# Compressing keys and values with two tokens in the contraction and two head groups side by side

## The chip, the cores and the metric

The kernel is one program on 1 core of a Trainium2 chip. The metric is the device time of one execution in microseconds (us). Times of a run are compared with those of the kernel before.

## The reference

One inference step of a two-layer decoder, for a prompt of 512 tokens and 8 sample sequences of 4 new tokens each, whose past of 256 tokens lies in pages of a cache. Layer 0 mixes tokens by retention and a spatial gate; layer 1 is sparse attention. One of its branches first compresses keys and values, and this is what the change touches:

```python
CMP_LEN, CMP_STRIDE = 32, 16        # NSA_KV = 4 groups, HEAD_DIM = 64
def compress(rows, pe_k, pe_v, phi_k, phi_v):      # rows: [k, v] of each token
    ...
    kb = blocks[:, :, :, 0] + pe_k[:, None, :]
    vb = blocks[:, :, :, 1] + pe_v[:, None, :]
    kc = jnp.einsum('bnlgd,lde->bnge', kb, phi_k)
    vc = jnp.einsum('bnlgd,lde->bnge', vb, phi_v)
    return kc, vc
```

A block is 32 consecutive tokens, and a new one begins every 16 tokens: 31 blocks in the prompt, 15 in each sample sequence (from its pages). For every group, each block is contracted over its 32 tokens `l` and 64 dims `d` with a kernel `phi[l, d, e]`. Everything is float32.

## The kernel before

Five engines run instruction streams that are written by hand, with semaphores between them. The order on each engine is the order of the code. Activations lie transposed (dims on partitions, tokens in columns), and the large products split each float32 into a high and a low part: ScalarE writes the high part of a weight unit (`split_hi`, tile `wH`), VectorE the low part (`split_lo`, `wL`), TensorE makes three products in fp32r. SyncE loads the weight units (`load_unit`) into `raw`, which has two slots: unit u is loaded once `wL` of unit u-2 is written. A product lands in one of two PSUM slots, `gemm`, which must be evacuated before it is used again.

The compression runs in two places.

**The sample sequences, in layer 0's output projection** (`project_out(E_OUT, 1, 1)`: 4 weight units, 8 chunks). Layer 1's cached pages are brought in here, beside layer 0's work. GpSimd loads 16 pages one by one (`load_page`): it reads a page number from the table, then issues a DMA of 256 KB. There are 4 page buffers. Before each chunk but the first, and after the last one, TensorE transposes two pages (`turn_pages`), 4 squares of 128x128 each; ScalarE copies them to `cT` (`take_pages`). SyncE loads the kernels `phiK`, `phiV` ahead of the last weight unit, after VectorE has cleared them: the two groups of a pair stand on a block diagonal of a 128x128 weight, so half of each weight is zeros. `compress(z, l0, l1)` then does one float32 matmul of 255 columns for each token place l (8 sequences, 2 pairs of groups, 15 blocks, and 15 columns for the position bias). Parts of `compress` stand among the steps of the norm that follows: behind the square sums of the projection, between the 8 square sums of the next norm (`square_sum(2, m, sqm)`), and around `spread_rstd(2)`, which sends the norm's factor to all partitions. VectorE then fills the input of the first feed-forward unit (`norm_fill`), piece by piece, and TensorE's `feature_chunk` waits for each piece.

**The prompt, in layer 1's input projection** (11 weight units from `O_IN`, each of 5 chunks for 5 tiles of tokens, but for one of gates). GpSimd clears `phiK2`, `phiV2` and loads them, behind two small tables and ahead of a copy of `win_sample` (4 MB from DRAM to DRAM). All six loads count on one semaphore, `o_in`. VectorE waits for it before its first rotary step, since that needs the tables `cosO` and `sinO`; `split_lo` of the next weight unit stands behind. After unit 3, TensorE transposes the prompt's rows (`turn_rows`), ScalarE copies them to `cPT`; after units 5 and 7 `compress_prompt(z)` does 32 float32 matmuls of 62 columns.

A float32 matmul shows as two records in the trace (two weight loads, two passes).

## Time and profile before

| | |
|---|---|
| median of 3 runs | 1756.84 us (1748.97 to 1760.66) |
| the profiled execution | 1754.42 us |
| its span, first to last instruction | 1752.6 us |
| mean granted TensorE clock | 0.959 of full speed |
| TensorE busy | 1622.1 us, 93% |
| VectorE, ScalarE, GpSimd busy | 781.5, 687.5, 228.5 us |
| moved by DMA | 140.56 MB, mean 80 GB/s |

The profiled execution takes 1.8 us more than its span, and lies 2.4 us under the median. In all views PE is TensorE's matmul stream and PEld its weight loads, DVE is VectorE, ACT ScalarE, POOL GpSimd, SP SyncE; a q behind it is the engine's sequencer. L801 is line 801 of the kernel before. Transposes are L556, VectorE's and ScalarE's helpers stand under one line each (L1499 the low parts, L1157 all of ScalarE's).

### The profile page before, as it was taken

What the parts mean: (1) busy time and instruction counts of PE and PEld (TensorE: products, weight loads), DVE (VectorE), ACT (ScalarE), POOL (GpSimd) and SP (SyncE); (2) the same over time, 40 slices, a digit from 0 to 9 for tenths busy, and PEclk for the clock granted to TensorE, in tenths of its full rate; (3) what the DMA queues carried; (4) which work ended last, traced back from release to release, by engine and by line L of the source; (5) the groups of instructions that cost most, each with busy time, mean ns of one, the idle gap of its engine ahead of it and who ended that gap; (6) DMA issues with size and microseconds to landing.
All of it is one profiled execution on the core that took longest, in us unless ns stands there. A gap on an engine that the chain in (4) does not pass through costs nothing.

```text
span 1752.6 us, 31047 instructions
## 1 busy us (share of the span) xinstructions
PE 1622.1 (93%) x12951; PEld 1483.6 (85%) x12951; DVE 781.5 (45%) x1251; ACT 687.5 (39%) x1303; POOL 228.5 (13%) x586
## 2 busy tenths in 40 slices
PE   4999988999999999978899889898869999999996
PEld 2989977799999999977899756565859999999995
DVE  2565453355542455343212366653236553255523
ACT  4123123345542455223222365655235553255422
POOL 3000001200000000002010344432100000000000
PEclk8999999999999999987999899999879999999998
DMA  6122318213323322324432210004211323332231
GB/s 207 49 74 96 97 55 170 83 29 92 87 78 107 82 76 78 90 86 86 174 112 59 51 50 1 1 1 145 59 48 49 96 73 95 89 96 74 72 88 51
DMA packets 189975, 140.56 MB, mean 80 GB/s; under 512 B 15505, under 2 KB 181665, under 8 KB 189809
## 3 DMA queue, kind: packets, MB, share of 16 engines
q1 hardware_dynamic: 179632, 107.36, 22.0%
q0 software_dynamic: 10240, 31.80, 6.4%
q8 instruction: 69, 1.13, 0.3%
q14 instruction: 34, 0.27, 0.0%
HBM read 130.32 MB, written 13.01 MB: 82 GB/s over the span
## 4 chain that ended last, share of the span: by engine, by line
PE 79%; DVE 8%; ACT 4%; DMA 4%; issue 3%; POOL 2%; POOLq 1%; SPq 0%; DVEq 0%; ACTq 0%
PE gemm L847 39%; PE gemm L581 17%; PE gemm L597 8%; PE misc L556 4%; PE gemm L982 1%; PE misc L1013 1%; DMA raw<-in_o_w_in 1%; ACT pr L1157 1%; POOLq L489 1%; DVE pr L1800 1%; DVE hL L1510 1%; DVE y L1527 1%; DVE y L1517 1%; PE misc L935 1%; PE misc L617 1%
## 5 line engine op out<-in xcount | busy, mean ns | idle before, releaser
L1499 DVE TENSOR_TENSOR wL<-raw,wH 128x2048 fp32r<-128x2048 f32 (+2 forms) x107 | 222.1, 2076 | 260.1 <-ACT wH L1157 260.1
L847 PE MATMUL gemm<-hH,wH 128*128 128x272 f32 x1280 | 268.4, 291 | 0.0
L847 PE MATMUL gemm<-hH,wL 128*128 128x272 f32 x1280 | 264.8, 288 | 0.0
L847 PE MATMUL gemm<-hL,wH 128*128 128x272 f32 x1280 | 264.0, 288 | 0.0
L1157 ACT ACTIVATE wH<-raw 128x2048 fp32r<-128x2048 f32 (+2 forms) x107 | 185.3, 1732 | 70.1 <-PE gemm L581 31.1
L847 PEld LDWEIGHTS gemm<-hH,wH 128*128 128x128 f32 x1280 | 200.6, 188 | 6.0 <-issue 5.0
L847 PEld LDWEIGHTS gemm<-hL,wH 128*128 128x128 f32 x1280 | 201.1, 188 | 0.0
L847 PEld LDWEIGHTS gemm<-hH,wL 128*128 128x128 f32 x1280 | 199.9, 189 | 0.0
L597 PE MATMUL gemm<-wH,hH 128*128 128x256 f32 x560 | 165.3, 295 | 15.6 <-DVE hL L1510 8.5
L1720 DVE SCALAR_TENSOR_TENSOR conv<-up,rows_t,conv 128x560 f32<-128x560 f32 x88 | 70.6, 802 | 218.4 <-ACT conv L1157 218.4
L597 PE MATMUL gemm<-wL,hH 128*128 128x256 f32 x560 | 162.9, 291 | 0.0
L597 PE MATMUL gemm<-wH,hL 128*128 128x256 f32 x560 | 161.7, 289 | 0.0
L581 PE MATMUL gemm<-hH,wH 128*128 128x272 f32 (+1 forms) x656 | 142.0, 298 | 7.5 <-DVE hL L1510 3.9
L581 PE MATMUL gemm<-hH,wL 128*128 128x272 f32 (+1 forms) x656 | 137.8, 292 | 0.0
L581 PE MATMUL gemm<-hL,wH 128*128 128x272 f32 (+1 forms) x656 | 137.7, 292 | 0.0
L1157 ACT ACTIVATE up<-gemm 128x32 f32<-128x32 f32 (+2 forms) x264 | 66.0, 324 | 175.9 <-PE gemm L847 154.4
L597 PEld LDWEIGHTS gemm<-wH,hH 128*128 128x128 f32 x560 | 109.9, 196 | 20.6 <-DVE hL L1510 7.2
L581 PEld LDWEIGHTS gemm<-hH,wH 128*128 128x128 f32 (+1 forms) x656 | 105.0, 192 | 13.6 <-issue 8.6
L597 PEld LDWEIGHTS gemm<-wH,hL 128*128 128x128 f32 x560 | 110.9, 198 | 0.0
L597 PEld LDWEIGHTS gemm<-wL,hH 128*128 128x128 f32 x560 | 110.2, 197 | 0.0
L847 PE MATMUL gemm<-aH,wH 128*128 128x272 f32 x528 | 110.2, 290 | 0.0
L847 PE MATMUL gemm<-aL,wH 128*128 128x272 f32 x528 | 108.9, 287 | 0.0
(332 smaller groups left out, 2720.5 us busy)
## 6 DMA issues: line engine op xcount, KB each, us to landing
raw<-in_f_w_in SPq DMA_DIRECT2D x88, 512.0 KB, 5.0
raw<-in_f_w_out SPq DMA_DIRECT2D x32, 704.0 KB, 4.6
raw<-in_e_w_in SPq DMA_DIRECT2D x12, 1024.0 KB, 5.1
raw<-in_o_w_in SPq DMA_DIRECT2D x10, 1024.0 KB, 5.2
raw<-in_e_w_out SPq DMA_DIRECT2D x4, 1024.0 KB, 6.2
pages<-in_cache_cmp POOLq DMA_DIRECT2D x16, 256.0 KB, 5.1
raw<-in_o_w_out SPq DMA_DIRECT2D x16, 256.0 KB, 5.7
rows<-in_cache_sel POOLq DMA_DIRECT2D x12, 256.0 KB, 3.0
```

The lines of the kernel that those rows point to most:

```text
L489: page = eng.value_load(a["page_table"][b:b + 1, pg:pg + 1], min_val=0, max_val=N_POOL - 1)
L556: ins = pe.transpose(out, in_, ident[base:base + k, base:base + k])
L581: ins = pe.matmul(gemm[c % 2][0:m, n, 0:TH], w, x[:, k, n * TH:(n + 1) * TH], start=(n_k == 0 and part == 0), stop=(n_k == nk - 1 and part ...
L597: ins = pe.matmul(gemm[c % 2][:, 0, 0:width], x, w, start=(k == 0 and part == 0), stop=(k == DC - 1 and part == 2))
L617: ins = pe.matmul(misc[:, 1 + q // 2, (q % 2) * TQ:(q % 2 + 1) * TQ], spread[:, q, :], rr[:, :], start=True, stop=True)
L847: ins = pe.matmul(gemm[odd][:, n, 0:TH], w, x[:, k, n * TH:(n + 1) * TH], start=(k == 0 and part == 0), stop=(k == nk - 1 and part == 2))
L935: ins = pe.matmul(b7[:, z * 2 * NCP:(z + 1) * 2 * NCP], (phiK2, phiV2)[z][:, l, :], cPT[:, 2 * z:2 * z + 2, l:l + 16 * (NCP - 1) + 1:16], ...
L982: ins = pe.matmul(slot[:, g2, 0:keys], qTs[j][half, r, rows], (ksT, kwT)[br][half, j, 0:keys], start=True, stop=True)
L1013: ins = pe.matmul(misc[64 * g2:64 * g2 + 64, 2 + grp % 2, r * P:(r + 1) * P], kvN[:, 1 + kt, (2 * br + 3) * 256 + g * HD:(2 * br + 3) * 25 ...
L1157: order(act.activation(out, in_, func, **kw), sem_)
L1499: order(dve.tensor_tensor(unit_view(wL, u), unit_view(raw, u), unit_view(wH, u).bitcast(F32), ALU.subtract), lo_ready)
L1720: order(dve.scalar_tensor_tensor(conv[:, j, :], U[:, j, 1:1 + CW], w[:, 17:18], conv[:, j, :], ALU.mult, ALU.add))
```

## The change

- `phiK`, `phiV`, `phiK2`, `phiV2` become [128 x 16 x 64]: the partitions hold two consecutive tokens' 64 dims. Nothing is zero, so nothing is cleared, and each is loaded by two DMAs of 256 KB in place of two of 512 KB. SyncE's loads wait for the barrier before the projection, no longer for VectorE.
- `compress` and `compress_prompt` go over 16 token pairs. For each pair two matmuls with 64 output columns follow each other, one for each group of the pair (`g2`), into partitions 0 to 63 and 64 to 127.
- A page is loaded to 64 partitions, two tokens on each, 4 KB per partition. VectorE copies the two pages of a sequence to `pairs`, so that one partition holds two tokens side by side; there are two slots. These 16 copies stand after `split_lo` of each of the 4 units. TensorE waits for `paired`, GpSimd reuses a page buffer after `paired`.
- Position tables: two DMAs in place of four.
- `turn_rows` uses four PSUM banks and waits for no copy; ScalarE makes 16 copies of 64x256 in place of 4 of 128x512.

```diff
-        phiK, phiV = sb("phiK", [P, CL, P]), sb("phiV", [P, CL, P])
-        cT = sb("cT", [P, 2, 16, 2 * DB + 1, 16])
-        pages = sb("pages", [P, 4, 512], at=top - 2 * FH * P * 4)
+        phiK, phiV = sb("phiK", [P, CL // 2, HD]), sb("phiV", [P, CL // 2, HD])
+        cT = sb("cT", [P, 2, 8, 2, 2 * DB + 1, 16])
+        pairs = sb("pairs", [P, 2, 2, G, 2 * HD])
+        pages = sb("pages", [P, 2, 2, 2, G, HD], at=top - 2 * FH * P * 4)
...
                 if u == E_OUT + 3:
-                    sp.wait_ge(phi_clear, 2)
+                    sp.wait_ge(phase, 2 * N_BAR)
                     for z, phi in enumerate((phiK, phiV)):
-                        name = ("o_phi_k", "o_phi_v")[z]
-                        for g in range(2):
-                            sp.dma_start(phi[64 * g:64 * g + 64, :, 64 * g:64 * g + 64], a[name][0].rearrange("l d e -> d l e")).then_inc(phi_in, 16)
+                        src = a[("o_phi_k", "o_phi_v")[z]][0].rearrange("(t l) d e -> l d t e", l=2)
+                        for l in range(2):
+                            sp.dma_start(phi[64 * l:64 * l + 64, :, :], src[l]).then_inc(phi_in, 16)
...
+                pe.wait_ge(paired, first // 2 + 1)
                 for n in (first, first + 1):
-                    pe.wait_ge(page_in[n % 4], 16 * (n // 4 + 1))
                     if n >= 2:
                         pe.wait_ge(page_ev, n - 1)
-                    for zj in range(4):
-                        turn(misc[:, 1 + n % 2, zj * P:(zj + 1) * P], pages[:, n % 4, zj * P:(zj + 1) * P], page_turned if zj == 3 else None)
+                    for g in range(G):
+                        turn(misc[:, 1 + n % 2, g * P:(g + 1) * P], pairs[:, (n // 2) % 2, n % 2, g, :], page_turned if g == 3 else None)
...
                 for l in range(l0, l1):
-                    ins = pe.matmul(out, (phiK, phiV)[z][:, l, :], cT[:, z, l % 16, :, l // 16:l // 16 + NCS],
-                                    start=(l == 0), stop=(l == CL - 1))
+                    for g2 in range(2):
+                        ins = pe.matmul(out[64 * g2:64 * g2 + 64, :], (phiK, phiV)[z][:, l, :], cT[:, z, l % 8, g2, :, l // 8:l // 8 + NCS],
+                                        start=(l == 0), stop=(l == CL // 2 - 1))
...
-            compress(0, 4, 8)
+            compress(0, 2, 4)
             for m in range(DC):
                 square_sum(2, m, sqm)
-                compress(0, 8 + 3 * m, 11 + 3 * m)
-            compress(1, 0, 8)
+                compress(0, 4 + 3 * m // 2, 4 + 3 * (m + 1) // 2)
+            compress(1, 0, 4)
             spread_rstd(2)
-            compress(1, 8, CL)
+            compress(1, 4, CL // 2)
...
                 for z in range(4):
-                    if z >= 2:
-                        pe.wait_ge(cp_ev, z - 1)
                     for t in range(4):
-                        turn(misc[:, z % 2, t * P:(t + 1) * P], kvN[:, t + 1, z * P:(z + 1) * P], cp_turned if t == 3 else None)
+                        turn(misc[:, z, t * P:(t + 1) * P], kvN[:, t + 1, z * P:(z + 1) * P], cp_turned if t == 3 else None)
...
-                for l in range(CL):
-                    ins = pe.matmul(b7[:, z * 2 * NCP:(z + 1) * 2 * NCP], (phiK2, phiV2)[z][:, l, :],
-                                    cPT[:, 2 * z:2 * z + 2, l:l + 16 * (NCP - 1) + 1:16], start=(l == 0), stop=(l == CL - 1))
+                for l in range(CL // 2):
+                    for g2 in range(2):
+                        ins = pe.matmul(b7[64 * g2:64 * g2 + 64, z * 2 * NCP:(z + 1) * 2 * NCP], (phiK2, phiV2)[z][:, l, :],
+                                        cPT[:, z, l % 8, g2, :, l // 8:l // 8 + NCP], start=(l == 0), stop=(l == CL // 2 - 1))
...
                     for z in range(4):
                         act.wait_ge(cp_turned, z + 1)
-                        activate(cPT[:, z, :], misc[:, z % 2, :], ACT.Copy, cp_ev)
+                        for g2 in range(2):
+                            tokens = misc[64 * g2:64 * g2 + 64, z, :].rearrange("p (u s l) -> p l s u", s=8, l=2)
+                            for l in range(2):
+                                activate(cPT[64 * l:64 * l + 64, z // 2, :, g2, z % 2, :], tokens[:, l, :, :], ACT.Copy, cp_ev if g2 and l else None)
...
                         dve.wait_ge(phase, 2 * N_BAR)
-                        for phi in (phiK, phiV):
-                            order(dve.memset(phi[:, :, :], 0.0), phi_clear)
-                        order(dve.memset(cT[:, :, :, 2 * DB, :], 0.0), pe_clear)
+                        for z in range(2):
+                            order(dve.memset(cT[:, z, :, :, 2 * DB, :], 0.0), pe_clear)
+                    if first == E_OUT:
+                        for b in (2 * i, 2 * i + 1):
+                            for n in (2 * b, 2 * b + 1):
+                                dve.wait_ge(page_in[n % 4], 16 * (n // 4 + 1))
+                            if b >= 2:
+                                dve.wait_ge(page_turned, 2 * (b - 1))
+                            for l in range(2):
+                                order(dve.tensor_copy(pairs[:, b % 2, :, :, HD * l:HD * l + HD], pages[:, b % 2, l]), paired if l else None)
...
                 if n >= 4:
-                    pool.wait_ge(page_turned, n - 3)
+                    pool.wait_ge(paired, n // 2 - 1)
                 page = pool.value_load(a["page_table"][n // NPG:n // NPG + 1, n % NPG:n % NPG + 1], min_val=0, max_val=N_POOL - 1)
-                pool.dma_start(pages[:, n % 4, :], a["cache_cmp"][0, page].rearrange("t z g d -> t (z g d)")).then_inc(page_in[n % 4], 16)
+                pool.dma_start(pages[64 * (n % 2):64 * (n % 2) + 64, (n // 2) % 2],
+                               a["cache_cmp"][0, page].rearrange("(t l) z g d -> t l z g d", l=2)).then_inc(page_in[n % 4], 16)
...
-            for phi in (phiK2, phiV2):
-                order(pool.memset(phi[:, :, :], 0.0))
-            order.wait()
             for phi, name in ((phiK2, "o_phi_k"), (phiV2, "o_phi_v")):
-                for g in range(2):
-                    pool.dma_start(phi[64 * g:64 * g + 64, :, 64 * g:64 * g + 64], a[name][0].rearrange("l d e -> d l e")).then_inc(o_in, 16)
+                src = a[name][0].rearrange("(t l) d e -> l d t e", l=2)
+                for l in range(2):
+                    pool.dma_start(phi[64 * l:64 * l + 64, :, :], src[l]).then_inc(o_in, 16)
```

VectorE at layer 0's output projection, before (wL<-raw,wH is `split_lo` of a weight unit, rr<-rq the norm's factor behind the projection; the names in brackets are the semaphores waited for):

```order
L1499 TENSOR_TENSOR wL<-raw,wH 128x2048 [waits hi_ready]
L1708 MEMSET phiK 128x4096 [waits phase]
L1708 MEMSET phiV 128x4096
L1709 MEMSET cT 128x32x16
L1499 TENSOR_TENSOR wL<-raw,wH 128x2048 [waits hi_ready] x3
L1505 RECIPROCAL rr<-rq 128x136 [waits rstd_ready,root_ready]
```

The same place now, up to the third weight unit:

```order
L1504 TENSOR_TENSOR wL<-raw,wH 128x2048 [waits hi_ready]
L1713 MEMSET cT 128x16x16 [waits phase]
L1713 MEMSET cT 128x16x16
L1721 COPY pairs<-pages 128x8x64 [waits page_in1,page_in0]
L1721 COPY pairs<-pages 128x8x64
L1721 COPY pairs<-pages 128x8x64 [waits page_in3,page_in2]
L1721 COPY pairs<-pages 128x8x64
L1504 TENSOR_TENSOR wL<-raw,wH 128x2048 [waits hi_ready]
L1721 COPY pairs<-pages 128x8x64 [waits page_turned,page_in1,page_in0]
L1721 COPY pairs<-pages 128x8x64
L1721 COPY pairs<-pages 128x8x64 [waits page_turned,page_in3,page_in2]
L1721 COPY pairs<-pages 128x8x64
```

The two large clears are gone, and the second to fourth low parts now stand behind waits for pages.

TensorE behind the projection, before (128x32 and 128x16 are the turned position tables; misc<-sqm is a square sum, misc<-rr the spread of the norm's factor):

```order
L556 MATMUL misc<-ident_sb,pe_in 128x32 x2
L556 MATMUL misc<-ident_sb,pages 128x128 x8
L610 MATMUL misc<-sqm,mean_d 32x136 x4
L801 MATMUL misc<-cT,phiK 128x255 x4
L617 MATMUL misc<-rr,spread_sb 128x136 x4
L801 MATMUL misc<-cT,phiK 128x255 x4
```

The same place now:

```order
L557 MATMUL misc<-ident_sb,pe_in 128x16 x2
L557 MATMUL misc<-ident_sb,pairs 128x128 x8
L611 MATMUL misc<-sqm,mean_d 32x136 x4
L803 MATMUL misc<-cT,phiK 64x255 x4
L618 MATMUL misc<-rr,spread_sb 128x136 x4
L803 MATMUL misc<-cT,phiK 64x255 x4
```

The count of matmuls and the number of columns that pass through stay, while each now fills 64 output rows, not 128. Between the square sums there were 3 matmuls, now 2 and 4 in turn.

GpSimd at the start of layer 1's input projection, before:

```order
L2019 DMA cosO<-in_cos_odd 128x40 [waits rows_stored,phase]
L2019 DMA sinO<-in_sin_odd 128x40
L2021 MEMSET phiK_132 128x4096
L2021 MEMSET phiV_133 128x4096
L2025 DMA phiK_132<-in_o_phi_k 64x32x64 [waits pool_chain]
L2025 DMA phiK_132<-in_o_phi_k 64x32x64
L2025 DMA phiV_133<-in_o_phi_v 64x32x64 x2
L2027 DMA out_win_sample<-in_state_win 8x8x16384
```

The same place now:

```order
L2031 DMA cosO<-in_cos_odd 128x40 [waits rows_stored,phase]
L2031 DMA sinO<-in_sin_odd 128x40
L2035 DMA phiK_133<-in_o_phi_k 64x16x64 x2
L2035 DMA phiV_134<-in_o_phi_v 64x16x64 x2
L2037 DMA out_win_sample<-in_state_win 8x8x16384
```

The kernels' loads follow the tables at once, and the 4 MB copy moves up by the two clears.

## Rows read from the trace of the kernel before

**Rows 1.** The page: the chain that ended last, by engine

```profile
PE 79%; DVE 8%; ACT 4%; DMA 4%; issue 3%; POOL 2%; POOLq 1%; SPq 0%; DVEq 0%; ACTq 0%
```

**Rows 2.** The chain in order of time, layer 0's output projection (start us, us, what)

```profile
269.19 2.80 DMA pages<-in_cache_cmp
...
272.04 1.12 PE misc L556 x4
273.15 7.42 PE gemm L581 x48
...
289.44 8.60 DMA pages<-in_cache_cmp
```

**Rows 3.** TensorE's timeline: the wait for that page (idle before, and its releaser, in brackets)

```profile
298.08 0.66 PE L556 MATMUL misc<-ident_sb,pages 128*128 128x128 f32 x4 [1.70 <-DMA pages<-in_cache_cmp]
```

**Rows 4.** GpSimd's timeline: the issue of the second page

```profile
269.19 0.56 POOL L1958 DMA_DIRECT2D pages<-in_cache_cmp  x1 [2.32 <-issue]
```

**Rows 5.** The chain behind the projection, to the first feed-forward chunk

```profile
329.72 1.99 PE misc L801 x8
...
332.67 1.47 DVE y L1527 x2
...
350.46 3.44 PE gemm L801 x16
...
354.82 10.32 PE gemm L801 x48
365.14 6.02 PE gemm L581 x48
```

**Rows 6.** TensorE's timeline, layer 1's attention: products of 64 output rows in pairs

```profile
1159.17 1.09 PE L1013 MATMUL misc<-pT_rows,kvN 128*64 128x128 f32 x16
1160.19 1.13 PE L982 MATMUL gemm<-kwT,qT 64*128 64x512 f32 x4
...
1224.78 1.19 PE L1072 MATMUL gemm<-kTs,qS 128*64 128x288 f32 x8
1225.80 0.65 PE L1125 MATMUL misc<-rows,pTs 128*64 128x128 f32 x8
```

**Rows 7.** The same steps in layer 1, without compression: chain in order of time

```profile
1296.68 1.47 DVE y L1527 x2
...
1312.61 0.79 DVE y L1517
...
1324.69 0.45 PE misc L556 x4
```

**Rows 8.** DMA issues from 276 to 290 us (issue, size, us to landing)

```profile
pages<-in_cache_cmp POOLq DMA_DIRECT2D x4, 256.0 KB, 7.2
```

**Rows 9.** VectorE: a copy of 128x512 (count: ns min/median/max)

```profile
L1609 DVE COPY qT<-misc x4: 691/692/692, 182.7 to 244.0; 128x512 f32<-128x512 f32 x4
```

**Rows 10.** The chain in layer 1's input projection

```profile
812.28 3.47 POOL phiV L2021
...
819.31 13.19 DMA phiV<-in_o_phi_v
...
836.58 22.53 DMA raw<-in_o_w_in
...
874.81 28.54 PE gemm L597 x240
903.36 7.12 PE misc L935 x64
```

**Rows 11.** TensorE's timeline there: the first matmul of the third weight unit

```profile
836.60 0.38 PE L597 MATMUL gemm<-wH,hH 128*128 128x256 f32 x1 [0.88 <-DVE wL L1499]
```

**Rows 12.** ScalarE's timeline there: evacuation of the last chunk of units 3 and 4

```profile
851.18 0.39 ACT L1157 ACTIVATE kvN<-gemm 128x256 f32<-128x256 f32 x1 [2.47 <-PE gemm L597]
...
872.58 0.39 ACT L1157 ACTIVATE kvN<-gemm 128x256 f32<-128x256 f32 x1 [2.47 <-PE gemm L597]
```

**Rows 13.** ScalarE's timeline, four copies of 128x256 from PSUM

```profile
283.64 1.19 ACT L1157 ACTIVATE cT<-misc 128x256 f32<-128x256 f32 x4
```

More of the change, by code:

```diff
@@ L288, in build_program @@
         O1 = place["at"]
-        phiK2, phiV2 = sb("phiK2", [P, CL, P]), sb("phiV2", [P, CL, P])
-        cPT = sb("cPT", [P, 4, SEQ])
+        phiK2, phiV2 = sb("phiK2", [P, CL // 2, HD]), sb("phiV2", [P, CL // 2, HD])
+        cPT = sb("cPT", [P, 2, 8, 2, 2, SEQ // 16])
         gT = sb("gT", [48, T], at=O1)
@@ L820, in project_out @@
                 if fill:
-                    compress(0, 0, 4)
+                    compress(0, 0, 2)
                 spread_rstd(n)
@@ L1246, in take_pages @@
                 if first == DB * NPG - 2:
-                    act.wait_ge(pe_clear, 1)
+                    act.wait_ge(pe_clear, 2)
                     act.wait_ge(pe_turned, 2)
-                    activate(cT[:, :, :, 2 * DB, 0:2], b7[:, 0:64].rearrange("p (z h l) -> p z l h", z=2, h=2), ACT.Copy, pe_ev)
+                    for g2 in range(2):
+                        activate(cT[:, :, :, g2, 2 * DB, 0:2], b7[:, 0:32].rearrange("p (z h s) -> p z s h", z=2, h=2), ACT.Copy, pe_ev if g2 else None)
                 for n in (first, first + 1):
-                    b, pg = n // NPG, n % NPG
+                    b, z = n // 2, n % 2
                     act.wait_ge(page_turned, n + 1)
-                    for z in range(2):
-                        activate(cT[:, z, :, 0:2 * DB, 8 * pg:8 * pg + 8].rearrange("p l (j b) u -> p j l b u", j=2)[:, :, :, b, :],
-                                 misc[:, 1 + n % 2, 256 * z:256 * z + 256].rearrange("p (j u l) -> p j l u", j=2, l=16), ACT.Copy, page_ev if z else None)
+                    for g2 in range(2):
+                        activate(cT[:, z, :, g2, 0:2 * DB, :].rearrange("p s (j b) u -> p j s b u", j=2)[:, :, :, b, :],
+                                 misc[:, 1 + n % 2, :].rearrange("p (j g u s) -> p g j s u", j=2, g=2, s=8)[:, g2], ACT.Copy, page_ev if g2 else None)
             def take_blocks(z):
@@ L1375, in _ @@
                         act.wait_ge(cp_turned, z + 1)
-                        activate(cPT[:, z, :], misc[:, z % 2, :], ACT.Copy, cp_ev)
+                        for g2 in range(2):
+                            tokens = misc[64 * g2:64 * g2 + 64, z, :].rearrange("p (u s l) -> p l s u", s=8, l=2)
+                            for l in range(2):
+                                activate(cPT[64 * l:64 * l + 64, z // 2, :, g2, z % 2, :], tokens[:, l, :, :], ACT.Copy, cp_ev if g2 and l else None)
                 elif n in (5, 7):
@@ L2019, in _ @@
                 pool.dma_start(dst, src).then_inc(o_in, 16)
-            for phi in (phiK2, phiV2):
-                order(pool.memset(phi[:, :, :], 0.0))
-            order.wait()
             for phi, name in ((phiK2, "o_phi_k"), (phiV2, "o_phi_v")):
-                for g in range(2):
-                    pool.dma_start(phi[64 * g:64 * g + 64, :, 64 * g:64 * g + 64], a[name][0].rearrange("l d e -> d l e")).then_inc(o_in, 16)
+                src = a[name][0].rearrange("(t l) d e -> l d t e", l=2)
+                for l in range(2):
+                    pool.dma_start(phi[64 * l:64 * l + 64, :, :], src[l]).then_inc(o_in, 16)
             win_out = o["win_sample"][0].rearrange("b s z g d -> b s (z g d)")
```

12 lines of the change are left out of this document (6 added, 6 removed).

## The prediction

> **What bounds the kernel now.** I read the chain that ended last first. It says that TensorE holds 79% of the end, DMA, GpSimd and waits of other kinds a few per cent each [rows 1], so a microsecond taken from TensorE is usually a microsecond gained, if what comes next on its engine is ready. Then I read the chain in order of time at the three places that the change touches. The reader is to see three things. In layer 0's projection TensorE waits for pages [rows 2, 3]. Behind it the compression itself is the chain, from 332.67 us to 365.14 us, with VectorE's 8 steps of the norm hidden under it [rows 5]. In layer 1's projection the chain leaves TensorE altogether: a clear of a kernel, its DMA, then the DMA of a weight unit, and only then TensorE again [rows 10].
>
> **Part 1, the sample compression.** It is 64 matmuls, 128 records. With 128 output rows a record of 255 columns costs 10.32 / 48 = 0.215 us [rows 5]. What do two neighbours of 64 output rows cost? Layer 1's attention has them: 8 records of 288 columns take 1225.80 - 1224.78 = 1.02 us, 0.128 each, where the 255 columns above already cost 0.215; 16 records of 128 columns take 1160.19 - 1159.17 = 1.02 us, 0.064 each [rows 6]. So the two halves do pass at the same time, and 255 columns should cost 0.128 x 255 / 288 = 0.113 us, half of now. (The Trainium skill, TensorEngine Tiling (Array Packing), Performance Considerations and Key Properties, promises up to 2x for two column tiles, but a drain whenever the tiling changes. Square sums of 32 rows stand between the parts here; by that drain the sum could lose something at each of some 20 changes. No row here isolates the drain, and the rows of the attention, which change tiling every microsecond, still show 0.064.)
>
> What is late next? Up to the norm's fill, VectorE. Layer 1 has the same steps with no compression between them: from VectorE's first step to the first step of the fill 1312.61 - 1296.68 = 15.93 us, and from there to the end of the first feed-forward chunk 1324.69 - 1312.61 = 12.08 us, 28.0 us in all [rows 7]. Layer 0 takes 365.14 + 6.02 - 332.67 = 38.5 us [rows 5]. TensorE has behind the last square sum 12 matmuls, 24 x 0.113 = 2.7 us, ahead of the spread; root and reciprocal take about as long beside it, so it is hardly later than in layer 1. The other 24 matmuls, 48 x 0.113 = 5.4 us, lie beside the fill of 11 us and cost nothing. **Gain 10.5 us**, between 9 and 11. That only half of the 14 us saved on 64 matmuls, and some more, is seen comes from VectorE taking over. The part ahead of the first spread, 1.99 us now [rows 5], halves: between 0 and 1.0, I take **0.6**, since the norm's factor is nearly ready then.
>
> **Part 2, pages and pairs, a loss.** The chunk behind the first page transposes starts at 273.15 [rows 2]. Now TensorE needs both pages and two copies. The second page is issued at 269.19 [rows 4] and landed 2.80 us later [rows 2]. But SyncE no longer waits for VectorE's two clears: its kernel loads go out with the barrier, ahead of the first page issues and some 12 us sooner, and pages issued beside them landed in 7.2 us in the median, 8.6 us at worst [rows 2, 8]. The loads are half the bytes, so they should be well on when the second page is issued; I take 6.0 us: landed at 275.2. The copies: 128x512 costs VectorE 0.69 us from PSUM [rows 9]; two of them at most 1.4, I take 1.2. Eight transposes at 1.12 us for four [rows 2]: 2.2 us. The chunk starts at 278.6 for 272.7 to 273.15, 5.9 us later. Bounds: landing 2.8 and copies 0.7 give 2.2 us later, landing 8.6 and copies 1.4 give 8.7. Given back: the wait of 1.70 us for a page that lay behind the kernel loads [rows 3], since these are over by then. **Loss 4.2 us**, between 0.5 and 7. The clears taken from VectorE hide under waits and count nothing. The 16 copies, 11 us of VectorE, stand ahead of the low parts of the weights, 1.4 us per pair, and I find about 1 us of room at each; the 32 ScalarE copies stay 32. (The Trainium skill, SBUF — State Buffer, Door 1: The DMA port swizzle, speaks against the new page layout: 64 partitions reach half of the ports, 196 in place of 328 GB/s for 1 MB. By that a page of 256 KB would take an estimated 0.5 us more; the trace of before has no page load of 64 partitions. Its section The "DVE blocks DMA" trap says that a float32 copy on VectorE holds up descriptors written by GpSimd; each copy is under a microsecond, so that estimate too is small.)
>
> **Part 3, the start of layer 1's projection.** The two clears, 3.5 us each, stand in the chain ahead of the kernel loads, and the last load took 13.19 us [rows 10]. VectorE's rotary step waits for it, then the low part of the third unit, for which TensorE idles 0.88 us [rows 11]. SyncE may load the fifth unit only then, at 836.58, into the 4 MB copy and the row output: 22.53 us [rows 10]. ScalarE stands at that unit's high part and doesn't evacuate, so the fourth unit takes 872.58 - 851.18 = 21.4 us [rows 12] where two take 28.54 [rows 10]: 7.1 us lost, part of it at the lower clock behind the stall. Now the loads go out 7 us sooner with half the bytes. The last is issued at 812.3 and lands at about 819 by half of 13.19, at 825.5 if it is no faster. The low part then directly follows its high part, some 10 us sooner, the fifth unit's load starts 10 us sooner, and even if it still takes 22.5 us it is there at 849, ahead of 851.5 when it is asked for. **Gain 8.0 us**, if that holds. The rest of the copy is a cover that is used up sooner, no loss.
>
> **Part 4, the prompt compression.** 64 records take 7.12 us [rows 10], 0.111 each for 62 columns, where 255 columns cost 0.215: it isn't the columns that bound, it is the load of 128 weight columns. With 64 output rows each load is half. Bounds: 0.064 with 128 columns [rows 6], and 62/128 of that, 0.031. I take 0.058, near the upper since the load stays the bound: 3.7 us for 7.12, twice: **gain 6.8 us**, between 6 and 10. (The Trainium skill, TensorE: Matmul & The Clock Gate, LDWEIGHTS, gives columns / 1.2 ns, 107 ns for 128: the trace agrees with 111. For 64 that is 53 ns, and the sum would be 7.4.)
>
> **Part 5, the prompt's copies.** ScalarE has 16 copies of 256 elements, 0.30 each by 1.19 us for four [rows 13], 4.8 us where there were some 2.4 (4 of 512 elements, as 8 of 256); behind them stand a high part of 1.9 us and an evacuation. TensorE can do two chunks of 2.85 us before it needs that evacuation, so it comes out even, 0 to 1 us. The wait that is removed was a fraction of a microsecond. I count **0.2 gained**.
>
> **The sum**, against the profiled execution of 1754.4 us: -10.5 - 0.6 + 4.2 - 8.0 - 6.8 - 0.2 = -21.9, 1732.5 us. The median of the runs lies 2.4 us above that execution, so I forecast 1735 us.
>
> **The rivals.**
> - *The halves don't overlap here.* For: their columns come from the same tile and all sums go to one PSUM bank. Against: so they do in the attention [rows 6]. Then parts 1 and 4 vanish, and 1756.8 + 4.2 - 8.0 gives 1753. Chance 0.07.
> - *The fifth unit's load is late anyway.* For: it now starts in the middle of the 4 MB copy, whose large packets slowed it before. Against: 2.5 us of room even at 22.5 us. Part 3 gives 0 to 2: 1742. Chance 0.15.
> - *The clock falls.* TensorE gets more idle in the norm of layer 0, and in layer 1's twin it ran at the lower level. If a chunk, its transposes and the next chunk run so, some 6 us come back: 1741. Chance 0.12.
> - *Pages set the pace, slower than before.* Two pairs are in flight; each needs two issues of 2.9 us [rows 4], a landing L, and 1.4 us of copies, behind which VectorE's low parts queue, and TensorE behind both. The pace is (7.2 + L) / 2 per chunk, against about 7.4 now (6.0 of products, 1.1 of transposes, a square sum), so it decides from L = 7.6. A landing of 8.6 costs 0.5 a chunk; all of the 22 us are eaten when 6 pairs cost 3.7 more each, at L = 15. For: the new layout halves the partitions of each page load. Against: outside of the kernel loads pages land in 2.8 us. 1762 us. Chance 0.05.
>
> **How the numbers follow.** The forecast has 0.61. Its own range is 1727 (page loss 0.5, the prompt at its lower bound) to 1741. The second and third rival lie just above; I take 1724 to 1750, which leaves out most of the first and the last. A measurement of this kernel tells about 1% from no change, so faster means under 1739.3: the forecast nearly whole, and a little of the second and third, 0.63. Within 1%: 0.33. Slower: 0.04.
>
> **What would show it.** In the changed kernel's profile: compression records of 255 columns about 0.11 us apart, of 62 columns under 0.064; the first page transposes late, near 276, and no later wait for pages; VectorE's first norm step to the end of the first feed-forward chunk about 28 us; VectorE's wait for the kernels in layer 1 gone, and no wait of ScalarE for `raw` there. It would be wrong if `split_lo` in layer 0 waits behind copies, if the fifth unit's load still lands late, or if the lower clock shows in the feed-forward.

## The result, and the profile after

The changed kernel takes 1740.25 us in the median of 14 runs (1733.43 to 1748.16), the kernel before 1753.17 us in as many: a ratio of 0.9925, 95% interval 0.9912 to 0.9938. A gain of 0.75%, 13 us; it is within the 1% that the prediction set as the bound of "faster". The forecast was 1735 us, the range 1724 to 1750. Two executions of the kernel before, of 2033.59 and 5257.46 us, lie far off all others and are left out of every figure.

| profiled execution | before | after |
|---|---|---|
| time, span | 1754.42, 1752.6 us | 1738.51, 1736.5 us |
| mean granted TensorE clock | 0.959 | 0.952 |
| TensorE, VectorE, ScalarE, GpSimd busy | 1622.1, 781.5, 687.5, 228.5 us | 1603.8, 780.4, 691.7, 218.7 us |

I read the views of before again at the same places. First the chain in order of time (start us, us, what) in layer 0's output projection and behind it, against [rows 2] and [rows 5]:

```profile
270.06 6.08 DMA pages<-in_cache_cmp
...
276.23 0.80 DVE pairs L1721 x2
277.08 1.97 PE misc L557 x8
279.05 6.46 PE gemm L582 x48
...
294.32 6.01 PE gemm L582 x48
...
301.73 6.00 PE gemm L582 x48
...
323.93 6.03 PE gemm L582 x48
...
335.15 1.47 DVE y L1532 x2
...
347.41 1.01 PE misc L803 x8
348.42 1.72 PE gemm L803 x16
...
351.30 0.79 DVE y L1522
...
361.55 1.84 PE gemm L582 x12
363.39 0.45 PE misc L557 x4
```

The first chunk starts at 279.05, 5.9 us later than in [rows 2], behind a page that took 6.08 us; the chunks then follow every 7.4 us, and the wait of [rows 3] is gone. Behind the projection 16 records of the compression take 1.72 us for 3.44 in [rows 5], the 48 records behind the spread are no longer in the chain, and VectorE is in their place (y at 351.30, its steps up to the last products of the chunk). From VectorE's first step to the end of the first feed-forward chunk it is 363.39 - 335.15 = 28.24 us, for 38.5 [rows 5].

Then layer 1's input projection, the chain again, against [rows 10]:

```profile
802.16 30.05 DMA raw<-in_o_w_in
832.23 1.91 ACT wH L1158
834.14 0.28 ACT kvN L1158
...
834.47 23.10 PE gemm L598 x192
857.57 0.45 PE misc L557 x4
...
864.50 1.91 ACT wH L1158
...
866.43 0.39 ACT kvN L1158
...
866.87 24.59 PE gemm L598 x192
891.46 2.01 PE misc L936 x64
...
915.26 2.02 PE misc L936 x64
```

The kernels have left the chain, and so has the fifth unit's load. But a load of a weight unit is still in it: the fourth unit's, issued at 802.16 and landed 30.05 us later. In the kernel before the same load was issued at 811.0 and landed in 5.2 us (the view of `raw` from 805 to 822 us):

```profile
L504 SPq DMA_DIRECT2D raw<-in_o_w_in x1: 368/368/368, 811.0 to 811.0; - x1
DMA to landing us min/median/max: 5.2/5.2/5.2
```

GpSimd's timeline now has the kernels' loads and the 4 MB copy right around its issue:

```profile
799.97 1.67 POOL L2035 DMA_DIRECT2D phiK<-in_o_phi_k  x2
801.62 1.64 POOL L2035 DMA_DIRECT2D phiV<-in_o_phi_v  x2
803.25 0.61 POOL L2037 DMA_DIRECT2D out_win_sample<-in_state_win  x1
```

TensorE's timeline (in brackets the idle time before and its releaser) has two waits here:

```profile
834.47 0.39 PE L598 MATMUL gemm<-wH,hH 128*128 128x256 f32 x1 [2.29 <-ACT kvN L1158]
...
866.87 0.45 PE L598 MATMUL gemm<-wH,hH 128*128 128x256 f32 x1 [1.84 <-ACT kvN L1158]
```

The first stands behind ScalarE's wait for that load, the second behind the prompt's copies. ScalarE's groups from 855 to 866 us (count, busy us, mean ns, idle before) show these:

```profile
L1158 ACT ACTIVATE cPT<-misc 64x256 f32<-64x256 f32 x16 | 6.1, 379 | 0.4
```

And 64 records of the prompt's compression take 2.01 us for 7.12 [rows 10].

The places add up. At the start of the prompt's first compression the changed kernel is 903.36 - 891.46 = 11.9 us ahead; the two compressions give 5.1 us each, so that it leaves the projection 22 us ahead, which is the sum that was forecast. At the end it is 16.1 us ahead (1752.6 - 1736.5), and over the runs 13. The stretches of the attention show where the profile lost 5 of the 6 (columns: stretch, length, busy us and count of TensorE's matmuls, its weight loads, VectorE, ScalarE, GpSimd, then the granted clock, DMA share and GB/s). After:

```profile
1070.00:1100.00 30.00, 28.14 (x176) 15.80 (x176) 14.93 (x72) 15.47 (x56) 12.01 (x25) 0.72 0.00 1
```

and the same place of the kernel before, which has 274 matmuls in the time of 176:

```profile
1075.00:1105.00 30.00, 27.30 (x274) 18.67 (x270) 18.03 (x75) 17.00 (x56) 13.72 (x26) 1.00 0.01 2
```

### The profile page after: what moved, and what is told of

The parts are those of the page before. It is cut to its first block, busy times and chain, and to the rows that moved or that the text cites. A ratio compares the mean times of both kernels' runs of the same rounds, so it can differ in the third digit from the quotient of the medians.

```text
span 1736.5 us, 31072 instructions
## 1 busy us (share of the span) xinstructions
PE 1603.8 (92%) x12951; PEld 1459.8 (84%) x12951; DVE 780.4 (45%) x1266; ACT 691.7 (40%) x1316; POOL 218.7 (13%) x582
## 4 chain that ended last, share of the span: by engine, by line
PE 79%; DVE 8%; ACT 5%; DMA 3%; issue 3%; POOLq 1%; POOL 1%; SPq 0%; DVEq 0%; ACTq 0%
PE gemm L849 40%; PE gemm L582 18%; PE gemm L598 9%; PE misc L557 5%; DMA raw<-in_o_w_in 2%; PE gemm L983 2%; PE misc L1014 1%; DVE y L1522 1%; DVE hL L1515 1%; ACT pr L1158 1%; DVE y L1532 1%; DVE pr L1812 1%; POOLq L490 1%; DVE xT L1536 1%; PE misc L618 1%
## 5 line engine op out<-in xcount | busy, mean ns | idle before, releaser
L849 PE MATMUL gemm<-aH,wL 128*128 128x272 f32 x528 | 108.9, 287 | 0.0
```

What stands on the lines that cost most here:

```text
L849: ins = pe.matmul(gemm[odd][:, n, 0:TH], w, x[:, k, n * TH:(n + 1) * TH], start=(k == 0 and part == 0), stop=(k == nk - 1 and part == 2))
```

## The experiments

Each line says what was timed beside the kernel before on the same chip. "Ahead" is how much sooner than in before's first profile TensorE starts the last part of layer 1's input projection, read by the position of the matmul in the stream, in one profile of each kernel; "lower clock" is the mean time of a run at the lower of the two levels (half of full speed), 2 x (1 - granted clock) x span, over the runs. The experiments were timed on four chips, so kernels from different chips are best compared by their ratios.

| kernel | median us | ratio, 95% interval | ahead, us | lower clock, us |
|---|---|---|---|---|
| before (67 runs beside the experiments) | 1752 to 1755 | 1 | 0 | 146 |
| before, again (1 run) | 1755.19 | not taken | 4.4 | 151 |
| after | 1740.25 | 0.9925 (0.9912 to 0.9938) | 21.9 | 159 |
| after, again | 1743.88 | 0.9950 (0.9929 to 0.9971) | 16.2 | 168 |
| prompt half alone | 1744.33 | 0.9951 (0.9932 to 0.9970) | 8.4 | 145 |
| sample half alone | 1750.58 | 0.9984 (0.9960 to 1.0008) | 8.2 | 161 |
| one half first | 1747.54 | 0.9979 (0.9961 to 0.9996) | 11.5 | 155 |
| kernels behind the first pair | 1733.23 | 0.9882 (0.9854 to 0.9910) | 19.8 | 142 |
| 4 MB copy last | 1743.10 | 0.9940 (0.9925 to 0.9955) | 25.8 | 174 |
| prompt's copies split | 1736.21 | 0.9906 (0.9871 to 0.9941) | 20.1 | 153 |
| copy behind the first rows | 1731.83 | 0.9871 (0.9845 to 0.9898) | 25.8 | 150 |
| kernels behind the pair, copies split | 1731.97 | 0.9860 (0.9833 to 0.9886) | 24.4 | 144 |
| all three | 1730.38 | 0.9857 (0.9831 to 0.9884) | 28.3 | 149 |
| before, copy moved | 1747.15 | 0.9976 (0.9963 to 0.9988) | 8.5 | 142 |

### The changed kernel and the kernel before, once more

No edit.

> The changed kernel once more. The sum of my terms was 22 us; the first profile is 16 us shorter than the one of before, and it is 22 us ahead at the end of layer 1's input projection, from where 5.8 us are lost again in attention, with a stretch of 17 us at the lower TensorE clock that the profile of before does not have. Theory A (the clock's fall in attention is chance and falls anywhere): this profile has its slow stretches elsewhere, and its lead over before at the start of attention is again 21 to 22 us. Theory B (the change brings it about): the same stretch is slow again, near 1075 us. Time 1738 to 1742 us either way.

> The kernel before once more, for its profile. The first profile of it has one short stretch of 3.4 us and one of 10.2 us at the lower TensorE clock in the sample attention near the end, the four profiles of changed kernels have more there and end 1 to 4 us less ahead than at its start. If the first profile was a lucky one, this one has 2 us or more added in that region; if the change brings the slow stretches about, it is as the first.

The changed kernel came out at 1743.88 us, 0.9950. Its interval just overlaps the first, so the gain is known to some 3 us and not better. The stretch at the lower clock near 1075 us wasn't there (its profile keeps its lead up to the last part of the attention, and loses 4 us in that, for which no run was made), while before's second profile had it, 17 us long near 1091, and lost 5.0 us in it. So that stretch isn't made by the change; it comes and goes. In the sample attention near the end, the place for which the second profile of before was taken, it added 1.1 us to the first, less than the 2 that I had set as a sign of a lucky first profile, so that question stays open.

One thing more is in before's second profile: at the end of layer 1's projection it is 4.4 us ahead of the first, though nothing was changed. Every figure of "ahead" hangs on the first profile and can't be trusted to better than that; differences between two parts of one profile are steadier.

### Each half of the change alone

`prompt_only` has the hunks of the diff on `phiK2`, `phiV2`, `turn_rows`, `compress_prompt` and `cPT`; `sample_only` has all the others.

> Only the prompt's half of the change (layer 1's input projection: kernel loads, turned rows, ScalarE's copies, compression); the sample's half as before. From the two profiles this half is worth 10.2 us of compression, 8.0 us of the old stalls, less 2.3 us for a weight unit that lands late and 3.1 us behind ScalarE's 16 copies: 12.8 us ahead of before at the end of the projection. My forecast had 15.0 for it. If the two halves lean on each other (for instance through when units are loaded), it is less than 11.

> Only the sample's half (layer 0's output projection, pages, pairs, norm). From the profiles: 2.6 us lost at the pages, 0.4 won ahead of the first spread, 10.3 won behind it: 8 us ahead of before at the feed-forward. My forecast had 6.9. The rival that TensorE's clock pays it back in the feed-forward would leave under 4.

The prompt half gives some 9 us, the sample half 3, with an interval that holds no gain at all. In the profiles each leaves the projection about 8 us ahead, and 8.4 + 8.2 = 16.6 lies within the 16.2 to 21.9 of the two profiles of the whole. For the sample half that is the 8 us that I expected; its time gained less than 4 us, though, as under the rival that the clock pays it back. The prompt half missed its 12.8 us and lies under the 11 that were to show that the halves lean on each other: its compressions gained their 10 us, but behind its late fourth load only 2.3 us of the old stalls were won by the time the rows are transposed, and behind the copies 3.1 were lost. The sample half spends 15 us more of each run at the lower clock than the kernel before (161 for 146), the prompt half none; that is where the two part. With the clears left in place, `sample_only` loads its fourth unit in 5.2 us and its fifth in 21 us, as before; `prompt_only`, without them, its fourth in 32.0 us.

### One half of the output rows first

The same matmuls, but the 16 token pairs of one group before those of the other, so that neighbours fill the same 64 rows:

```diff
-                for l in range(l0, l1):
-                    for g2 in range(2):
+                for g2 in range(2):
+                    for l in range(l0, l1):
```

and the same in `compress_prompt`.

> The changed kernel with the two loops exchanged: all token pairs of one half of the output rows, then all of the other, in each call of the compression. Same instructions, same bytes; only neighbours now share a half of the array. If the gain is the overlap of two halves, records of 255 columns go back from 0.11 to 0.21 us apart and of 62 columns from 0.031 to 0.05 to 0.06 (the load of 64 weight columns then binds); the kernel is 10 to 14 us slower than the changed one, about level with before. If the gain came from the smaller weights alone, it stays within 3 us of the changed one.

The chain in order of time:

```profile
346.69 1.02 PE misc L803 x8
...
350.05 2.62 PE gemm L803 x16
...
353.80 9.66 PE gemm L803 x48
```

```profile
898.42 3.69 PE misc L936 x64
```

48 records of 255 columns take 9.66 us, 0.201 each, where the two halves in turn have 1.72 / 16 = 0.108 and the kernel before 0.215 [rows 5]. So the records are shorter because the two halves overlap; smaller weights alone would have left them near 0.2. The order matters only in long runs of one half, though. Between the square sums this kernel does 4 records of one half and then 4 of the other, and these 8 take 1.02 us, as long as in turn (1.01); 8 and 8 take 2.62 us for 1.72, and only the 24 and 24 come near the kernel before. At each change of half 0.7 to 0.8 us are saved against 0.215 a record. The prompt is different: 3.69 / 64 = 0.058 a record with neighbours in the same rows, half of the 0.111 of 128 output columns [rows 10], and 2.01 / 64 = 0.031 in turn, half again. With 128 weight columns the load is the bound, since the time halves with the weight columns while the 62 columns stay. With 64 the two can't be told apart: by 0.215 us for 255 columns, 62 take 0.052. But half of 0.111 is 0.056, and 0.031 a record is less, so in turn the loads of the two halves overlap too.

I expected this order to be 10 to 14 us slower, level with the kernel before. It is slower by 3.7 us than the changed kernel on the same chip (1747.54 for 1743.88) and by 7 us than its first median: the records between the square sums, 48 of the sample compression's 128, lost nothing.

### The kernels' loads behind the first pair

SyncE sends the loads of `phiK`, `phiV` only when the first pair of pages has been copied:

```diff
-                    sp.wait_ge(phase, 2 * N_BAR)
+                    sp.wait_ge(paired, 1)
```

> The changed kernel, with SyncE's loads of phiK and phiV put behind the first pair of pages (it waits for the first copy to `pairs`) in place of the barrier. If the pages land late because they share the DMA engines with these loads, the second page lands in about 3 us and not 6.1, and the second chunk of layer 0's projection starts 3 us sooner; the same chunk is then about 3 us behind the kernel before and not 5.9. If the 64-partition layout makes pages slow, it still takes 6 us. The later pages may take 6 to 8 us each then; by my count there is room. Time 0 to 3 us better than the changed kernel.

The chain:

```profile
269.20 3.28 DMA pages<-in_cache_cmp
272.57 0.77 DVE pairs L1721 x2
273.39 1.97 PE misc L557 x8
275.36 6.56 PE gemm L582 x48
```

The second page lands in 3.28 us for 6.08, and the chunk starts at 275.36 for 279.05; no page is late afterwards. So the kernels' loads beside it were what slowed the page, 2.8 us here (in the other profiles that have these loads beside the page it took 6.04 to 9.05 us). The runs gain more, 7 us or more against the changed kernel: they spend at least 17 us less at the lower clock, and the wait of TensorE behind which its clock is low is 8.40 us long, not 11.88. In the projection of layer 1, though, the lead over the changed kernel's first profile, 3.1 us at the end of the first feed-forward chunk, is gone (19.8 us ahead of before for 21.9): the fourth unit's load now takes 32.4 us, and its wait takes back what came in sooner.

### The 4 MB copy last

GpSimd issues the copy of `win_sample` just ahead of the barrier before the attention.

```diff
-            pool.dma_start(win_out[:, 0:PAST, :], a["state_win"]...)
...
+            pool.dma_start(win_out[:, 0:PAST, :], a["state_win"]...)
             meet(pool, order, 3)
```

> The changed kernel, with the 4 MB copy of win_sample moved from the start of layer 1's input projection to just ahead of attention. In the changed kernel the fourth weight unit of that projection lands 30 us after its issue (5 us before the change) and stalls ScalarE and TensorE, by 2.3 us in one profile and more in two others. If the copy is what slows it, it lands in under 10 us here, no unit waits, and the projection ends 2 to 6 us sooner. If the kernel loads and the row output are enough, it still lands after 20 us or more. Time 2 to 6 us better than the changed kernel, if attention doesn't pay for the copy.

The fourth unit's load takes 11.2 us in place of 30.0, ScalarE doesn't wait for it, and the kernel leaves the projection 25.8 us ahead, 3.9 more than the changed one. But the time is no better, because of the attention. The chain of what held GpSimd:

```profile
950.30 0.61 POOL out_win_sample L2073
950.91 26.42 issue
...
977.48 0.61 POOL pr L2081
```

The barrier stands behind the copy on GpSimd, and GpSimd passes it only when the copy has landed, 25.1 us after its issue. That takes 10 us of the lead. The theory on the load held; the new place was wrong.

### The prompt's copies shared with VectorE

VectorE does half of the 16 copies to `cPT` (tiles 2 and 3 of the four), between the low part of the fifth unit and its next rotary step:

```diff
-                    for z in range(4):
+                    for z in range(2):
                         act.wait_ge(cp_turned, z + 1)
...
+                if n == 3:
+                    for z in range(2, 4):
+                        dve.wait_ge(cp_turned, z + 1)
+                        ... dve.tensor_copy(cPT[64 * l:64 * l + 64, z // 2, :, g2, z % 2, :], tokens[:, l, :, :])
```

> The changed kernel, with 8 of ScalarE's 16 copies of the prompt's rows (those of keys and values' second half of groups) given to VectorE, which idles there. If it is these copies that stall TensorE after the fourth unit (16 in 6.4 us, then a high part of 1.9 us, then the evacuation that TensorE waits for; 3.1 us lost), TensorE waits for no evacuation and the loss is gone. If the transposes or the banks are what costs, nothing changes. Time 3 us better than the changed kernel.

ScalarE's and VectorE's timelines:

```profile
863.38 3.20 ACT L1158 ACTIVATE cPT<-misc 64x256 f32<-64x256 f32 x8
```

```profile
864.25 3.60 DVE L1773 COPY cPT<-misc 64x256 f32<-64x256 f32 x8 [11.00 <-PE misc L557]
```

TensorE's second wait, 1.84 us, is gone. 1736.21 us against 1740.25 and 1743.88: some 4 to 8 us, at the edge of what four runs tell.

### The copy behind the first row output, and the sums

```diff
-            pool.dma_start(win_out[:, 0:PAST, :], a["state_win"]...)
...
             store_rows(0, cmp_rows_out)
+            pool.dma_start(win_out[:, 0:PAST, :], a["state_win"]...)
```

> The 4 MB copy of the window cache is issued behind the first row output (near 828 us) in place of 803 us. If the copy is what slows the fourth unit's load of layer 1's input projection (30.0 us from issue to landing), that load lands in 5 to 12 us, ScalarE's wait of 5.3 us for it goes and TensorE's 2.3 us with it; the fifth unit's load then runs beside the copy and takes some 20 us, but has about 28 us until ScalarE asks for it, so no new wait; layer 1's projection ends 2 to 4 us earlier than in the changed kernel: 1737 us. Rival: the kernel loads, now sent in the same moment, slow it, not the copy; then it still takes over 20 us and the time stays at 1740. Second rival: the fifth unit is late in its place, as before the change: 1742 or more.

> The kernel loads of layer 0 behind the first pair, and half of the prompt's 16 copies on VectorE. If the two are independent, their gains against the changed kernel add: the first page transposes at 273.4 us in place of 277.1, and no stall of TensorE for the evacuation behind the copies (1.8 us and the lower clock behind it): 7 + 4 = 11 by the times of the single edits, 1730 us. Rival: much of what each gained was time at the lower clock, which is shared: no better than the better one of the two, 1733.

> Both of those and the copy behind the first row output. If each of the three waits costs for itself: 1730 - 3 = 1727 us, some 26 us under the kernel before, and at the end of layer 1's projection its profile is 26 to 29 us ahead of that of before. Rival: as above, 1733; or the moved copy meets the load of the fifth unit and ScalarE, which now has fewer copies, waits for it: 1730 or above.

Of the copy behind the first rows, the view of the DMAs into `raw` issued from 822 to 838 us, and the chain:

```profile
L505 SPq DMA_DIRECT2D raw<-in_o_w_in x1: 367/367/367, 831.1 to 831.1; - x1
DMA to landing us min/median/max: 26.3/26.3/26.3
```

```profile
798.18 56.92 PE gemm L598 x462
```

The fourth unit's load takes 12.0 us for 30.0. The fifth's, now beside the copy, takes 26.3 us from 831.1, lands at 857.4, and ScalarE asks for it at 862.03: no wait. TensorE does 462 matmuls without a pause where it had one. 1731.83 us, 8 to 12 us less than the changed kernel, for 3.9 us of lead in the projection. The fifth load took 26.3 us where I expected some 20, and the time is 5 us better than the 1737 that I expected. The runs have 9 to 18 us less at the lower clock than the changed kernel's (150 for 159 and 168), which would account for 3 to 6 us by the estimate below; no run shows that it does.

The two other edits together give 1731.97 us, no more than the better of the single ones (1733.23) by the interval. Here is why, in the chain and in TensorE's timeline of that kernel:

```profile
797.39 34.23 DMA raw<-in_o_w_in
...
831.65 1.91 ACT wH L1158
```

```profile
833.88 0.58 PE L598 MATMUL gemm<-wH,hH 128*128 128x256 f32 x1 [6.84 <-ACT kvN L1158]
```

The load is issued 4.8 us sooner than in the changed kernel and lands at the same moment, 831.6 for 832.2. TensorE waits 6.84 us for it in place of 2.29. What was gained ahead of that load is lost at it in this profile. With all three moves TensorE has no wait from 800 to 893 us:

```profile
797.61 57.18 PE gemm L598 x462
854.79 1.75 PE misc L557 x16
856.54 28.54 PE gemm L598 x240
```

The lead is 28.3 us, and the time 1730.38 us, 1.4% below before; the 1727 us that I expected, each wait costing for itself, were not reached. That is the fastest kernel of the study, although its interval doesn't part it from the two with fewer moves.

### The copy moved in the kernel before

Nothing of the change; the 4 MB copy stands behind the second row output.

> The kernel before, with the 4 MB copy of the window cache issued behind the second row output (near 870 us) in place of 820 us, and nothing of the change. If the copy is what made the fifth unit's load late there (22.5 us from issue to landing), the load takes 5 to 12 us, ScalarE's wait of 7.56 us for it goes, and the fourth unit is done in 14.3 us in place of 21.4: 7 us sooner at the end of layer 1's projection, 1747 us, so that 7 of the change's 17 to 18 us could have been had without it. Rival: the load is late because it is issued late, behind VectorE's wait for the kernels, and the kernel loads lie in its way; then most of the wait stays: 1752 or more. The copy beside the later units' loads has its own risk: a new wait of ScalarE near 889 or 910 us.

The chain:

```profile
818.03 13.05 DMA phiV<-in_o_phi_v
...
835.18 28.84 PE gemm L597 x240
```

The fifth unit's load takes 8.3 us for 22.53 [rows 10], the wait for it is gone, and 240 matmuls run without a pause where [rows 10] has the load. It is 8.5 us ahead at the projection's end and 5.2 us faster in the median (0.9976). The last load of the kernels still takes 13.05 us for 13.19, so the copy had no part in that. Some 5 to 8 of the microseconds of the change could have been had by moving one line.

## Why the prediction was right, and where it was not

**Part 1, the sample compression: right.** Forecast 28.0 us from VectorE's first step to the end of the chunk, measured 28.24; forecast 0.113 us a record, measured 0.108; VectorE took over as the last to be ready. The rival that the halves don't overlap fell by the records, and the long runs of one half in the order with one half first show what that world looks like. The rule of the Trainium skill on array tiling (TensorEngine Tiling (Array Packing), Key Properties) that a change of tiling drains the array has no new price here: between square sums of 32 rows 8 records take 1.01 us, 0.15 more than at 0.108 each, and in the kernel before 6 took 1.49 us there, 0.20 more than at 0.215 each.

**Part 2, pages: right in what happens, the loss somewhat too large.** The chunk started at 279.05, where 278.6 was forecast, 5.9 us later than in [rows 2]. Landing 6.08 us for 6.0, copies 0.80 for 1.2, transposes 1.97 for 2.2, and the page issued 0.9 us later than before. Of the 6.1 us of the landing, 2.8 were the kernels' loads, since behind the first pair they left 3.28. By the fourth chunk the changed kernel is only 3.0 us late (301.73 against the end of the transposes in [rows 3], 298.74), 4.4 in its second profile, for 4.2 in the sum. The 1.70 us of [rows 3] that I counted as given back are no fixed cost: before's second profile has no wait there. The rival that pages set the pace fell: the chunks follow every 7.4 us.

**Part 3, the start of layer 1's projection: the step that failed.** I wrote that "the fifth unit's load starts 10 us sooner" and isn't late: true, it landed in 20.5 us and nobody waited. But I looked only at the load that was late before. In the kernel before the fourth unit's load was issued at 810.96, and GpSimd, busy with the clears until 815.75 [rows 10], sent its own loads and the copy only from 816.03 on, as it landed. Without the clears, all five go out between 799.97 and 803.25 us, and the fourth unit's load is among them: 30.05 us. ScalarE waited 5.34 us for it and TensorE 2.29. I had named the 4 MB copy as a cover used up sooner, "no loss", and missed that the clears were a cover themselves. The experiments split the 30 us: with the copy moved away 11.2 to 12.0 us, with the clears left in (`sample_only`) 5.2 us. So the copy costs 18 of them, the kernels' loads 6 to 7. The term came to 7.2 us for 8.0 in the profile and 3.8 in the second one; with the copy moved it is 9.8, in the prompt half alone 2.3, and in the kernel before with nothing but the copy moved 8.3.

**Part 4, the prompt compression: right mechanism, undersized.** 64 records in 2.01 us, forecast 3.7: a gain of 5.1 twice, 10.2 us in place of 6.8 (its upper bound was 10). I took the value near the bound of a load of 64 columns; one half first showed just that, 0.058. With the halves in turn the loads overlap as the columns do, and the lower bound that I had, 0.031 by the columns alone, was the answer. The Trainium skill's figure (TensorE: Matmul & The Clock Gate, LDWEIGHTS), 53 ns for 64 columns, fits the 0.058 of neighbours in the same rows, though the columns alone would take about as long there, and is not the pace of two halves in turn, 0.031.

**Part 5, the prompt's copies: too small.** 0.40 us each from one start to the next, not 0.30, so 6.4 us for 4.8. "It comes out even" was wrong: TensorE waited 1.84 us and ran at the lower clock behind it, about 3 us in all, and the 0.2 us of gain weren't there. I had priced a copy of 64x256 that reads every second element by one of 128x256 in order.

**The sum and the rivals.** By the lead at the end of each part, the profile has 7.8 us for Parts 1 and 2 (forecast 6.9), 7.2 for Part 3 (8.0), -3.1 for Part 5 (0.2) and 10.0 for Part 4 (6.8): 21.9 us, as forecast. That is luck twice over. One error covered another, and the first profile of before is the slower of two at this place: against the second, the changed kernel's two profiles are 17.5 and 11.8 us ahead. The second profile of the changed kernel has 5.5, 3.8, -3.1 and 10.0 against the first of before: 16.2.

The runs show 10 to 13 us, little more than half of the forecast gain. The time of 1740 lies near 1735 also because I counted from 1756.84 us, a median of three runs, and 14 runs of the same kernel gave 1753.17. The call that I had given 0.63, faster than 1739.3 us, did not come; within 1%, which had 0.33, did.

Part of the gap is the clock. The runs spend 13 to 22 us more at the lower level than before (159 and 168 for 146). What this costs can be estimated from the 67 runs of the kernel before, which do the same work each time: their time rises by 0.35 us per us at the lower level (correlation 0.84). By this estimate it is 5 to 8 us, and at equal clocks the two kernels would differ by 18 us (13.4 + 4.6 and 9.9 + 7.7, from the mean times). None of it was in my sum. That the sample half brings the lower clock is shown by the halves (161 and 145 us). The profiles show where part of it lies. From 262 to 300 us, around the wait for the first pages, the granted clock is 0.91 in both profiles of before, 0.87 and 0.82 in those of the changed kernel (TensorE idle for 11.88 and 12.63 us), 0.82 in the sample half's, and 0.91 again with the loads behind the pair (8.40 us idle; with all three moves it is 0.87 at 8.56 us). So 3 to 7 us of it come with the longer wait. The rival "the clock falls" held in one place more: from 330 to 366 us the clock is 1.00 in the first profile of the changed kernel but 0.95 in the second, as in eight of the ten profiles that have the sample half and in none of the four without. These 3.4 us lie among the steps of the norm; the feed-forward chunk behind them ran at the full clock in every profile. Where the rest lies differs from profile to profile, and its cause is open.

## What to carry to other kernels

A step that is removed from one queue may have been what kept that queue's next transfers away from another's: before costing it at its duration, list every DMA that it lets go earlier, and every load that will then be in flight with them, not only the one that was late before. Float32 products with 64 output rows are best issued with the two halves in turn, or in short runs of each (4 records took no longer here, 8 did), which halved the time of a record. And an improvement ahead of a late load can be taken back at the load, so that small moves should be tried together. A profile of the kernel before is one draw: take a second one before reading a lead of a few microseconds.

## What the runs showed of the hardware that was not expected

- Weight loads of 64 columns into the two halves of the array overlap: 0.031 us a record in turn, 0.058 in one half, 0.111 for 128 columns, all float32 with 62 columns.
- Products of the two halves overlap in short runs as well: 4 records of one half and 4 of the other took 1.02 us, strictly in turn 1.01.
- A load of 1 MB took 5.2 us with neither beside it, 11 to 12 us beside four loads of 256 KB of kernels issued in the same 3 us, and 30 to 34 us when a copy of 4 MB within DRAM was in flight too. Issued 4.8 us earlier, with the kernels and the copy as much earlier, it landed at the same moment in the one profile that has this.
- GpSimd, with its barrier behind a copy, stood still for 26.4 us, until the copy had landed (25.1 us from its issue), though its wait for the copy's semaphore comes only later in its code.
- In one place of the attention the clock of TensorE falls in one profile and not in the next: of either kernel one profile had 17 us at the lower level there and another none.
